# Attention steps of a hybrid decoder: P.V right behind the scores, fourteen projection passes in one run, the shift row as a 64-row operand

## The reference, cut to what matters

```python
c = jnp.cumsum(lf, axis=1)                       # per head
s = jnp.einsum('bqhd,bkhd->bhqk', qi, k).astype(jnp.float32) * dh ** -0.5
s = s + ci[..., None] - c_keys[:, :, None, :]    # forget sums of query and key
s = jnp.where(mask, s, NEG_INF)                  # causal
p = jax.nn.softmax(s, axis=-1).astype(v.dtype)
return jnp.einsum('bhqk,bkhd->bqhd', p, v)       # 8 heads of 64
```

## Time and profile before

| | us |
|---|---|
| median of 3 runs | 1890.67 |
| lowest, highest | 1890.24, 1895.3 |
| profiled execution | 1893.1 |
| its span | 1891.4 |
| TensorE busy in the span | 1803.2 |
| VectorE, ScalarE, GpSimd busy | 730.6, 363.3, 502.5 |

### The profile page before, as it was taken

How to read it: one execution, slowest core, us unless ns; L and a number is a source line. 1 busy time by engine, 2 the same in 40 slices (tenths; PEclk the granted TensorE clock), 3 DMA queues, 4 the chain that set the end, 5 groups by cost and what they waited for, 6 DMA issues and landing times.

```text
span 1891.4 us, 29215 instructions
## 1 busy us (share of the span) xinstructions
PE 1803.2 (95%) x11360; PEld 1632.1 (86%) x11360; DVE 730.6 (39%) x1303; ACT 363.3 (19%) x691; POOL 502.5 (27%) x295
## 2 busy tenths in 40 slices
PE   5999999998999999999999989999999999999994
PEld 5966666665777879999999979999999999999993
DVE  3156766542415443121138754223213313312318
ACT  3132222322413223111120340100000010010022
POOL 3310101100210303332234524223232233322225
PEclk8999999998987979999999989999999999999997
DMA  5134434302642201111112212111111111111102
GB/s 155 54 108 122 118 116 117 122 25 80 180 143 47 56 8 50 44 44 54 46 34 72 63 34 59 54 44 44 44 44 53 36 55 44 44 46 54 45 23 90
DMA packets 173120, 126.39 MB, mean 67 GB/s; under 512 B 22266, under 2 KB 146570, under 8 KB 173042
## 3 DMA queue, kind: packets, MB, share of 16 engines
q1 hardware_dynamic: 169490, 124.09, 22.3%
q10 hardware_dynamic: 3552, 1.25, 0.3%
HBM read 115.45 MB, written 9.85 MB: 66 GB/s over the span
## 4 chain that ended last, share of the span: by engine, by line
PE 88%; DVE 5%; issue 2%; DMA 2%; ACT 2%; POOL 1%; SPq 1%; POOLq 0%; ACTq 0%; DVEq 0%
PE psum L741 14%; PE psum L745 14%; PE psum L744 14%; PE psum L819 4%; PE psum L825 4%; PE psum L823 4%; PE psum L1277 4%; PE psum L1276 4%; PE psum L1272 4%; PE psum L974 4%; PE psum L947 2%; PE psum L1225 2%; PE psum L1229 2%; PE psum L1228 2%; PE psum L950 1%
## 5 line engine op out<-in xcount | busy, mean ns | idle before, releaser
L689 POOL CAST wh<-raw 128x1024 fp32r<-128x1024 f32 x132 | 143.5, 1087 | 1342.9 <-PE psum L819 436.4
L741 PE MATMUL psum<-xh,wh 128*128 128x344 f32 (+1 forms) x1488 | 478.6, 322 | 6.5 <-POOL wl L691 3.6
L745 PE MATMUL psum<-xh,wl 128*128 128x344 f32 (+1 forms) x1488 | 476.4, 320 | 0.0
L744 PE MATMUL psum<-xl,wh 128*128 128x344 f32 (+1 forms) x1488 | 476.2, 320 | 0.0
L691 POOL TENSOR_TENSOR wl<-raw,wh 128x1024 fp32r<-128x1024 f32 x132 | 328.8, 2491 | 10.6
L741 PEld LDWEIGHTS psum<-xh,wh 128*128 128x128 f32 x1488 | 280.8, 189 | 7.6 <-issue 7.3
L744 PEld LDWEIGHTS psum<-xl,wh 128*128 128x128 f32 x1488 | 280.8, 189 | 0.2
L745 PEld LDWEIGHTS psum<-xh,wl 128*128 128x128 f32 x1488 | 280.7, 189 | 0.0
L2320 DVE TENSOR_TENSOR hf<-sg,psum 128x344 f32<-128x344 f32 x66 | 33.8, 513 | 385.0 <-PE psum L745 385.0
L819 PE MATMUL psum<-xh,wh 128*128 128x352 f32 (+1 forms) x480 | 164.0, 342 | 1.1 <-DVE negc_tok L1840 1.1
L823 PE MATMUL psum<-xl,wh 128*128 128x352 f32 (+1 forms) x480 | 161.2, 336 | 0.0
(11 more groups left out here) (305 smaller groups left out, 2621.8 us busy)
## 6 DMA issues: line engine op xcount, KB each, us to landing
raw<-in_w_in SPq DMA_DIRECT2D x86, 256.0 KB, 3.3
parts<-in_cache_k SPq DMA_DIRECT2D x64, 256.0 KB, 3.0
parts<-in_cache_v SPq DMA_DIRECT2D x64, 256.0 KB, 2.9
raw<-in_w_gate SPq DMA_DIRECT2D x44, 256.0 KB, 3.1
raw<-in_w_up SPq DMA_DIRECT2D x44, 256.0 KB, 3.2
raw<-in_w_down SPq DMA_DIRECT2D x44, 256.0 KB, 2.7
raw<-in_w_o SPq DMA_DIRECT2D x28, 256.0 KB, 3.0
cb<-negc_scratch SPq DMA_DIRECT2D x8, 520.0 KB, 5.3
```

The source lines that it names most:

```text
L689: pool.tensor_copy(wh[:, s, :], raw[:, r, :]).then_inc(sem("panel_high"), 1)
L741: first = mm(out, w[0], x[0], start=(n == 0), stop=False)
L744: mm(out, w[0], x[1], start=False, stop=False)
L745: last = mm(out, w[1], x[0], start=False, stop=(n == len(ks) - 1))
```

## The change

Three edits. The shift pair takes 64 rows of `onesr` and `nmT` instead of 2; both are made 128 partitions tall and zeroed at the start, so that the added rows add nothing. In the step's loop `mix(g-1)` moves ahead of the first seven passes, and with it the value round in the last pair; the order is then scores, piece at place 0, P.V, value round, seven passes, piece at place 1, sample sums, seven passes. Where nothing stands at place 1 the fourteen passes are one run. Nothing else moves; PSUM banks, semaphores and transfers stay.

```diff
-        onesr = keep("onesr", [DH + 2, P], F32R)
+        onesr = keep("onesr", [P, P], F32R)
...
-        nmT = c("nmT", [DH + 2, 2, SEG], F32R)
+        nmT = c("nmT", [P, 2, SEG], F32R)
...
             pool.wait_ge(made, 10)
+            pool.memset(f(onesr[:, :]), 0.0).then_inc(made, 1)
+            pool.wait_ge(made, 11)
             pool.tensor_copy(onesr[0:2, :], ones[0:2, :]).then_inc(made, 1)
             pool.tensor_copy(onesr[DH:DH + 2, :], ones[DH:DH + 2, :]).then_inc(made, 1)
-            pool.wait_ge(made, 12)
+            pool.wait_ge(made, 13)
...
                 for h, b in enumerate(ST_BANKS):
-                    rows = slice(DH * h, DH * h + 2)
+                    rows = slice(DH * h, DH * h + DH)
                     last = mm(psum[0:w, b, 0:n], onesr[rows, 0:w], nmT[rows, par, off:off + n], start=False,
                               stop=not diagonal)
...
+            def fill():
+                for _ in range(HALF_SLICE):
+                    next(filler, None)
+
...
                 maxima_at(j, x, 0)
-                for _ in range(HALF_SLICE):
-                    next(filler, None)
                 if g >= 1:
                     mix(g - 1)
+                if j == 3 and x in ROUNDS_AT:
+                    value_round(ROUNDS_AT[x])
+                fill()
                 maxima_at(j, x, 1)
                 if j == 3:
                     for u in SUMS_AT.get(x, ()):
                         sample_sums(u)
-                    if x in ROUNDS_AT:
-                        value_round(ROUNDS_AT[x])
-                for _ in range(HALF_SLICE):
-                    next(filler, None)
+                fill()
...
             link(ve.memset(nmax[:, :, 0, :], 0.0))
+            link(ve.memset(f(nmT[:, :, :]), 0.0))
             dve.wait_ge(sem("fz_ready"), 3)
```

More of the change, by code:

```diff
@@ L943, in tile_scores @@
                 diagonal = c0 == P * t
-                for a, b_, start in ((kh, qh, True), (kh, ql, False), (kl, qh, False)):
+                for a, b_, begins in ((kh, qh, True), (kh, ql, False), (kl, qh, False)):
                     for h, b in enumerate(ST_BANKS):
                         rows = slice(DH * h, DH * h + DH)
-                        mm(psum[0:w, b, 0:n], a[rows, keys], b_[rows, queries], start=start, stop=False)
+                        mm(psum[0:w, b, 0:n], a[rows, keys], b_[rows, queries], start=begins, stop=False)
                 for h, b in enumerate(ST_BANKS):
-                    rows = slice(DH * h, DH * h + 2)
+                    rows = slice(DH * h, DH * h + DH)
                     last = mm(psum[0:w, b, 0:n], onesr[rows, 0:w], nmT[rows, par, off:off + n], start=False,
```

## The result

The changed kernel takes 1868.35 us (median of 4 runs) against 1890.45 us of the kernel before (4 runs, the earlier three among them): a ratio of 0.9868, 95% interval 0.9854 to 0.9882. Run again later beside other kernels it took 1864.50 against 1892.70 us, a ratio of 0.9856 (0.9837 to 0.9876). The forecast was 1865.8, a gain of 24.9 us; the medians give 22.1 the first time and 28.2 the second, so the times bear the forecast out to within some 3 us and no closer.

What follows compares the result with a forecast made beforehand. The attention stage was taken as bound by TensorE's start times. Savings of 17.0, 5.3, 3.0, 1.0 and 1.1 less 2.5 us of growing waits gave 24.9 us off the 1890.67 us median: 1865.8 us, range 1860 to 1875.

Steps and rivals of the forecast that it cites:

- The 64-row form: Shift pair in all attention steps: on 64 rows it avoids entry and exit costs between matmul forms; 17.0 us saved.
- the second rival: Shift pair: the number of rows doesn't matter, its distances stay at 0.21 and 0.32 us; 1881 us, chance 0.07.
- One run of fourteen passes: Attention steps: P.V behind the scores spares one entry and exit of a projection run per step; 5.3 us saved.
- The k_tok waits and the clock: Step 16, first three pairs: P.V covers the wait for VectorE's copy, 3.0 us; second pair's P.V at full clock, 1.0.
- Value rounds: Last pair: six passes move behind round 1, within the time round 2's load needs; 1.1 us saved.
- round 2's wait: Last pair's second value round: TensorE's 2.54 us wait for a cache load should fall to near 1.5.
- Growing waits: Steps 5, 6 and 12: shorter steps meet a VectorE no faster; 2.5 us lost, bounds 0 and 8.
- the first rival: Pairs with cached keys: VectorE becomes the bound, costing 6 us more; 1872 us, chance 0.12.
- The third (clock at the boundaries): Rival: at all three pair boundaries the clock falls, costing 1 to 1.5 us each; 1869 to 1870 us, chance 0.10.
- the fifth (clock in the steps): Rival: small tiles without a full pass between lower the clock mid-step; slower, 1903 us at 20% of the stage, chance 0.02.
- scores to shift: Sign within a step: start distance from score pair to shift pair 0.13 us instead of 0.21.
- the length of step 11: Sign in the second pair: this step takes 4.5 us instead of 4.95.

Runs made afterwards that it cites:

- order_only: Changed kernel with the shift pair back on 2 rows, leaving the new order of a step alone; 1880.17 us, 0.9933 of the kernel before.
- table_sums: Changed kernel with cached-key parts placed by a table, forget sums loaded ahead of key loads, sample sums right behind P.V; 1862.54 us, again 1863.26.
- rows32: Changed kernel with the shift pair on 32 rows instead of 64; 1878.86 us, 0.9934 of the kernel before.
- rows48: Changed kernel with the shift pair on 48 rows instead of 64; 1869.50 us, 0.9884 of the kernel before.
- shift_only: Kernel before with the shift pair on 64 rows alone, old order of the steps kept; 1879.36 us, 0.9933 of the kernel before.
- pieces_first: table_sums with the piece of the maxima's scores right behind the shift pair, ahead of the tile's mask; 1856.22 us, 0.9817 of the kernel before.

## Why the prediction was right

The time lay within the range, 2.6 us over the value. The mechanism was the predicted one; that the sum came so close is partly luck, since terms that were too low and too high offset each other. The sum by terms, against what the runs show:

- **The 64-row form: 17.0.** Right. With waits left out, the steps of the first three pairs are 4.4 us a pair longer in order_only than in table_sums, and steps 0 to 13 of the last pair 3.2 us longer than in the changed kernel: 16.4, without the last pair's last steps. That the form and not the pair's other properties costs, the open point behind the second rival, is what rows32 and rows48 settled.
- **One run of fourteen passes: 5.3.** Slightly low. order_only's third pair, without waits for the maxima, is 2.6 us shorter than before, 1.0 of it the k_tok wait: 1.6 a pair, 6.4 in all.
- **The k_tok waits and the clock: 3.0 and 1.0.** Right in size: step 16 fell by 1.22, 2.61 and 1.21 us in the three pairs, 0.2 to 0.3 of each by the forms; some 4.3 together. The clock's part of it, 1.4 us, was there to be won only because the clock had fallen at one boundary of the profiled execution before. In shift_only it fell at none, with the same three waits. In the changed kernel it fell at none either, but that the shorter wait is the reason is not shown.
- **Value rounds: 1.1.** Wrong. The prediction took the six passes behind round 1 as new cover for round 2's load. But rounds 0 to 3 are held by their loads: from round 0 to 3 it is 18.2 us before and in order_only, 18.9 in the changed kernel and 18.0 when it ran again. Most of the 0.9 between the last two is clock: in the one it is 0.52 from 439 to 441 us, behind round 2's wait, and round 2 takes 1.80 us; in the other it stays at 1.00 there (436 to 439 us), and the round takes 1.04. Passes that moved between the rounds gained nothing; what came (0.8 us from step 14 to round 3, 1.7 the second time) is round 0 starting 1.5 us earlier in its step. I read round 2's wait alone; the distances of all four rounds would have told.
- **Growing waits: -2.5.** The term that was mis-sized. Against the lengths without waits (table_sums) the changed kernel loses 5.5 us in the first three pairs, the kernel before about 1.1: -4.4, within the bounds of 0 and -8. Their places, x = 5, 6 and 12, were named; but I sized them by VectorE's slack in one pair. The second pair has 3.6 of the 5.5, by two loads that wait in the queue for VectorE's progress and take as long as before (the second load of the forget sums is used 7.4 us after its issue, before 7.3) while the steps got shorter. This is the first rival in small, with loads as well as VectorE's own work behind it. A further part, which the prediction did not have, is VectorE's product standing behind GpSimd: the one of 2.96 us lies in step 11 of the first pair, which is 0.24 us longer than without it.

With the last pair's steps 14 to 16, which are 0.5 us shorter with everything in them, it is 16.4 + 6.4 + 4.3 + 0.5 - 4.4 = 23.2, against 23.3 in the stage. The second rival fell by rows32 and rows48. The third (clock at the boundaries) and the fifth (clock in the steps) didn't happen: the three pairs have 1.00. Of the marks the prediction gave, scores to shift, shift to piece, mask to P.V, the length of step 11 and the k_tok wait came as said; round 2's wait was 1.97, not 1.5.

## What to carry to other kernels

In a kernel bound by TensorE, read the distances between starts where one kind of matmul follows another, not only the durations: here a change of form and back (64-row pairs, 32-row pairs, full rows, 64 columns) costs about 0.2 us, and padding an operand with zeros and moving P.V gave 1.3 to 1.4%, with pieces_first's further moves 1.8%. Before such a gain is banked, list the loads and the other engines' work that are paced by steps: each shorter step brings them nearer, and here 3.6 of the 5.5 us of waits lay in the one pair with two late loads.

## What the runs showed of the hardware that I had not expected

- The cost of a 2-row operand pair depends on a threshold between 32 and 48 rows and not on the rows themselves: 32 rows 0.22 and 0.32 us in and out, 48 rows 0.12 and 0.22. Zero rows up to the neighbours' form cost no time: 0.12 us for the shift pair of 64 rows, as for a score pair.
- Between the bf16 mask of full rows and a projection pass the change is cheap: 0.10 us to the pass and 0.24 to the next, where behind the 2-row pair it is 0.32 and 0.26. Out of a 64-row pair it costs the same to either type: 0.21 us from a shift pair of 256 columns to the mask, 0.21 from one of 272 columns to P.V. That fits a form which does not depend on the type; no run tests it.
- VectorE's product of two large operands does not run beside GpSimd's split of a panel: begun during it, it ended about 1.1 us behind it, whatever was left, and took up to 3.4 us instead of 1.22.
- The same wait does not always cost the clock: six waits of 1.16 to 1.17 us for k_tok (three in the kernel before, three in shift_only) were followed by a granted clock of 0.50 once.
